# Expert products of a decoder trunk: column groups of 64 and 32 slots with plain fp32 weights in place of a three-product split

## The reference, cut to what matters

```
gu = xb @ w_gu[e] + b_gu[e]                  # 1024 -> 1024 (512 gate, 512 up)
gt = minimum(gu[:, :512], 7.0)
up = clip(gu[:, 512:], -7.0, 7.0)
act = gt * sigmoid(1.702 * gt) * (up + 1.0)
y = act @ w_down[e] + b_down[e]              # 512 -> 1024
```

## Time and profile before

| | |
|---|---|
| median of 3 runs | 1056.94 us (1056.68 to 1283.42) |
| the profiled execution | 1057.93 us |
| its span | 1056.1 us |
| TensorE busy | 996.8 us, 94% |
| VectorE busy | 778.8 us, 74% |
| ScalarE busy | 559.8 us, 53% |
| granted TensorE clock over the span | 0.98 |
| bytes moved by DMA | 283.35 MB |

### The profile page before, as it was taken

One profiled execution on the slowest core, in us unless ns is written; L12 is line 12 of the kernel. 1 busy time (PEld: TensorE's weight loads), 2 busy tenths in 40 slices (PEclk: granted clock), 3 DMA queues, 4 the chain that ended last, 5 costly groups with the idle time before them and its releaser, 6 DMA issues.

```text
span 1056.1 us, 13850 instructions
## 1 busy us (share of the span) xinstructions
PE 996.8 (94%) x4523; PEld 671.3 (64%) x4523; DVE 778.8 (74%) x1121; ACT 559.8 (53%) x840; POOL 215.2 (20%) x237
## 2 busy tenths in 40 slices
PE   3889999999999987899999999999999999999995
PEld 2566666667787557666666666666666666666652
DVE  0374967535534555898898898889989889898885
ACT  6334454452223233755575666756666665766742
POOL 1223931105100012212211212121122221212110
PEclk9899999999999998999999999999999999999998
DMA  9826624512316456889899999999999999999745
GB/s 343 297 81 239 239 81 168 188 43 70 118 69 239 159 206 235 307 310 316 307 332 370 360 370 366 351 373 359 369 357 354 377 354 363 368 365 363 245 126 195
DMA packets 63213, 283.35 MB, mean 268 GB/s; under 512 B 7489, under 2 KB 8797, under 8 KB 38601
## 3 DMA queue, kind: packets, MB, share of 16 engines
q1 hardware_dynamic: 53528, 257.93, 65.4%
q0 software_dynamic: 9648, 24.94, 8.9%
HBM read 272.62 MB, written 18.56 MB: 276 GB/s over the span
## 4 chain that ended last, share of the span: by engine, by line
PE 90%; DVE 5%; ACT 2%; issue 1%; DMA 1%; POOL 0%; ACTq 0%; SPq 0%; DVEq 0%
PE ps L1843 33%; PE ps L1578 19%; PE ps L1903 10%; PE ps L1897 9%; PE ps L1777 2%; PE ps L1607 2%; PE ps L1788 2%; PE ps L1626 2%; PE ps L1814 2%; PE ps L1692 2%; PE ps L1821 1%; PE ps L1864 1%; PE ps L1877 1%; DVE attn L1425 1%; DMA X<-in_x_dram 1%
## 5 line engine op out<-in xcount | busy, mean ns | idle before, releaser
L1843 PE MATMUL ps<-whl,xhl 128*96 128x512 f32 x1536 | 369.0, 399 | 0.0
L1307 DVE TENSOR_TENSOR whl<-ring,whl 128x1024 fp32r<-128x1024 f32 x256 | 304.4, 1221 | 52.5 <-ACT whl L965 51.8
L1843 PEld LDWEIGHTS ps<-whl,xhl 128*96 128x96 f32 x1536 | 249.8, 163 | 108.3 <-issue 0.2
L965 ACT ACTIVATE whl<-ring 128x1024 fp32r<-128x1024 f32 x256 | 268.2, 1061 | 63.7 <-PE ps L1843 43.9
L1578 PE MATMUL ps<-h_hi,wb_hl 128*128 128x512 f32 x384 | 127.1, 404 | 1.2 <-POOL wb_hl L652 1.2
L1903 PE MATMUL ps<-X,attn 128*96 128x512 f32 x256 | 115.4, 593 | 0.0
L733 POOL DMA_INDIRECT moe_rows<-mix,ius x31 | 46.3, 1493 | 304.8 <-ACT WC L1034 153.1
L1897 PE MATMUL ps<-whl,ahl 128*96 128x512 f32 x384 | 98.8, 407 | 2.9 <-DVE whl L1307 2.9
L1578 PEld LDWEIGHTS ps<-h_hi,wb_hl 128*128 128x128 f32 x384 | 72.9, 190 | 22.4 <-issue 5.2
L1307 DVE TENSOR_TENSOR whl<-X,whl 128x1024 fp32r<-128x1024 f32 x64 | 78.3, 1225 | 8.9 <-ACT whl L965 8.1
L965 ACT ACTIVATE whl<-X 128x1024 fp32r<-128x1024 f32 x64 | 67.8, 1062 | 20.0 <-PE ps L1843 20.0
(11 more groups left out here) (251 smaller groups left out, 1178.5 us busy)
## 6 DMA issues: line engine op xcount, KB each, us to landing
ring<-in_w_gu_dram SPq DMA_DIRECT2D x128, 1024.0 KB, 10.5
X<-in_w_down_dram SPq DMA_DIRECT2D x64, 1024.0 KB, 10.4
ring<-in_w_ada_dram SPq DMA_DIRECT2D x12, 2048.0 KB, 11.9
ring<-in_w_in_dram SPq DMA_DIRECT2D x6, 2048.0 KB, 7.8
ring<-in_w_out_dram SPq DMA_DIRECT2D x2, 2048.0 KB, 7.9
X<-in_x_dram SPq DMA_DIRECT2D x1, 2048.0 KB, 8.1
ring<-in_w_b_up_dram SPq DMA_DIRECT2D x1, 2048.0 KB, 14.8
ring<-in_w_a_up_dram SPq DMA_DIRECT2D x1, 2048.0 KB, 8.0
```

Source lines behind the costliest of these rows:

```text
L965: nc.scalar.activation(whl[:, buf, 0, :], part, ACT.Copy).then_inc(hi_ok, 1)
L1307: v.tensor_tensor(whl[:, buf, 1, :], part, whl[:, buf, 0, :], ALU.subtract).then_inc(lo_ok, 1)
L1843: last = mm(ps[0:slots, half, :], xhl[:, a, k, :], whl[:, at, b, half * CH:(half + 1) * CH], start=False, stop=(k == KD - 1 and a == 1))
```

## The change

An expert's products are all plain fp32, and nothing is split: `hi_part`, `lo_part`, `rows_low`, `act_low` and the ring `whl` are gone. The 96 slots are cut into 64 and 32. The first 64 are multiplied in two column groups of TensorE side by side (slots in output partitions 0 to 63 for one half of the columns, 64 to 127 for the other, 512 columns each), the last 32 in four groups (256 columns each). Each waits for a 1 MB half, does both of its blocks for the 64 slots, then both for the 32:

```diff
+            def up_pair(q, w):
+                w = w.rearrange("p (k u g c q) -> p k g c u q", k=2, u=2, g=2, c=2)
+                for i in range(2):
+                    k = 2 * q + i
+                    for g in range(2):
+                        mm(ps[SA * g:SA * (g + 1), 0, :], xgT[:, k, 0:SA], w[:, i, g, :, :, :], start=False,
+                           stop=(k == KD - 1), tile_position=(0, SA * g))
+                for i in range(2):
+                    k = 2 * q + i
+                    for j in range(4):
+                        last = mm(ps[SB * j:SB * (j + 1), 1, 0:2 * P], xgT[:, k, SA:slots], w[:, i, j // 2, j % 2, :, :],
+                                  start=False, stop=(k == KD - 1), tile_position=(0, SB * j))
+                return last
...
-                    for a, b in ((0, 0), (0, 1), (1, 0)):
-                        for half in range(2):
-                            last = mm(ps[0:slots, half, :], xhl[:, a, k, :], whl[:, at, b, half * CH:(half + 1) * CH],
-                                      start=False, stop=(k == KD - 1 and a == 1))
-                    last.then_inc(granule_used, 1)
```

`down_pair` does the same for the down weights, `biases` adds the bias once per group (2 matmuls of 512 columns, 4 of 256). Gate and up values now lie on 128 partitions x 384 columns instead of 96 x 512, so the three VectorE steps and the sigmoid run over 384 columns, and `turn_act` turns three 128 x 128 pieces. The result is weighed in six pieces:

```diff
-                for half in range(2):
-                    sl = slice(half * CH, (half + 1) * CH)
-                    last = v.scalar_tensor_tensor(out=Y[0:slots, b, sl], in0=ps[0:slots, 2 + half, :],
...
+                for g in range(2):
+                    sl = slice(g * CH, (g + 1) * CH)
+                    v.scalar_tensor_tensor(out=Y[0:SA, b, sl], in0=ps[SA * g:SA * (g + 1), 2, :], scalar=WC[0:SA, b:b + 1],
...
+                for j in range(4):
+                    sl = slice(j * 2 * P, (j + 1) * 2 * P)
+                    last = v.scalar_tensor_tensor(out=Y[SA:slots, b, sl], in0=ps[SB * j:SB * (j + 1), 3, 0:2 * P],
```

The weights have sixteen 1 MB places (`half_home`) in one ring, gate-up and down alike, and a place is free when its products are done (`half_used`). The rows of a down half are taken so that each partition gets two pieces of 4 KB instead of one of 8 KB:

```diff
-            dn = w_down[0, bass.ds(e, 1), :, :].rearrange("a (p k) n -> p (a k n)", k=KF)
-            return dn[:, q * PAIR:(q + 1) * PAIR]
+            dn = w_down[0, bass.ds(e, 1), :, :].rearrange("a (k p) n -> p (a k) n", k=KF)
+            return dn[:, 2 * q:2 * q + 2, :]
```

More of the change, by code:

```diff
@@ L553, in _, with refill @@
[L553 to L564 removed]
+            def refill(e, r):
+                for q in range(4):
+                    sp.wait_ge(half_used, up_no(e, q) - NH + 1)
+                    load_up(e, q, r * PER - 2 + q)
+                for q in range(2):
+                    sp.wait_ge(half_used, down_no(e - 1, q) - NH + 1)
+                    load_down(e - 1, q, r * PER + 2 + q)
@@ L1816, in turn_rows, with biases @@
                 last.then_inc(done, 1)
-            def biases(e, half):
+            def biases(b):
                 pe.wait_ge(b3_ok, 1)
-                mm(ps[0:slots, half, :], sel3[:, bass.ds(e, 1)].broadcast_to([3 * NE, slots]), b3[:, half * CH:(half + 1) * CH],
-                   start=True, stop=False)
-            def up_whole(e, done):
-                for half in range(2):
-                    biases(e, half)
-                    for k in range(KD):
-                        last = mm(ps[0:slots, half, :], xgT[:, k, :], gu_part(0, k)[:, half * CH:(half + 1) * CH], start=False,
-                                  stop=(k == KD - 1))
-                    last.then_inc(done, 1)
@@ new lines, in came, with up, down @@
+            def came(n, rounds):
+                pe.wait_ge(half_in[n % NH], rounds * 48 + n // NH * 16 + 16)
+            def up(e, r, rounds=0):
+                biases(r % 2)
+                for q in range(4):
+                    n = q if isinstance(e, int) and e == 0 else r * PER - 2 + q
+                    came(n, rounds)
+                    up_pair(q, half_home(n)).then_inc(half_used, 1)
+            def down(e, r, rounds=0):
+                for q in range(2):
+                    n = down_no(e, q) if isinstance(e, int) else r * PER + 8 + q
+                    came(n, rounds)
+                    down_pair(q, half_home(n)).then_inc(half_used, 1)
@@ L1953, in _ @@
                         pe.wait_ge(ov_w, n * 96 + 96)
-                        up_whole(e, ov_gu)
+                        biases(0)
+                        for q in range(4):
+                            last = up_pair(q, half_home(q))
+                        last.then_inc(ov_gu, 1)
                         pe.wait_ge(ov_av, n + 1)
@@ L1957, in _ @@
                         pe.wait_ge(ov_at, n + 1)
-                        down(ov_dn)
+                        for q in range(2):
+                            last = down_pair(q, half_home(4 + q))
+                        last.then_inc(ov_dn, 1)
                 pe.wait_ge(ov_y, OVER * NE)
```

367 lines of the change are left out of this document (139 added, 228 removed).

## The result

The changed kernel takes 1064.16 us (median of 6 runs, 1062.65 to 1069.28), the kernel before in the same comparison 1057.34 us (median of 6). One run of the kernel before took 1283.42 us and is left out of the ratio, which compares the means of the others: 1.0074, with a 95% interval of 1.0044 to 1.0103, within 2%, though not nothing. The profiled execution of the changed kernel is its slowest, 1069.28 us with a span of 1067.5; against the span of 1056.1 before there are 11.4 us to find.

A forecast was written before the change was run, and what follows sets the result against it. TensorE was taken to set the pace, with DMA also full. Period +10.3, places waits -2.6 and tail -3.0 gave +4.7 us: 1062.6 on the profiled execution, forecast 1062 us, range 1012 to 1095 us.

The forecast's parts named there:

- The period: TensorE's time per expert in the loop: 19.05 us against 18.72, +10.3 us over 31 periods and the last gate-up.
- rival D: Column groups in TensorE's products don't run fully side by side: 320 us more, or 1187 us in a milder form; chance 0.04.
- B (cheap changes): The 12 changes between 64 and 32 per expert don't drain TensorE: 17.85 us per expert, 1024 us; chance 0.28.
- C: At each of 16 changes TensorE's next group waits for the last record's whole tail, 0.16 us: 1092 us; chance 0.20.
- The sum without changes: TensorE's products, biases and transposes per expert, before any cost for changing group size: 16.74 us.
- The places products wait 0.65 us for VectorE in experts 1 to 4: At the loop's start, these TensorE waits were taken as gone with the splits: -2.6 us.
- The tail: From the last gate-up's end to the last weighing: products and turning -4.9 us, weighing +1.9, net -3.0 us.
- The weighing grows from two pieces to six, but nobody waits for it until the tail: Weighing of each expert's result: hidden in the loop, 3.2 us against 1.41 in the tail, +1.9 us.
- The bound on the 4 KB pieces: Down-half loads in 4 KB instead of 8 KB pieces: between no loss and 0.3 us per expert.
- DMA could follow no faster for long: In the kernel before, DMA was held to be full too, at share 1.00 and 363 GB/s, while TensorE set the pace.
- The floor of 17.5 us: DMA's least time per expert, with loads running ahead: remaining 203 MB take 559 us at 363 GB/s.
- What stays hidden: Activation steps, 3.8 us, stay covered by TensorE's transposes and 5.7 us of down products; losing that costs some 2 us per expert.

The follow-up runs named there:

- the direct pair: Changed kernel without the 32 slots' products, down halves in 4 KB pieces against 8 KB pieces: 1019.15 and 1001.42 us.
- the three together: Changed kernel with pairs in turned order (11 changes), TensorE's loop written out and the last expert's result in its own banks: 1031.93 us, ratio 0.9763.
- the other two edits: Against the changed kernel, tried singly: TensorE's expert loop written out, 1059.73 us; last expert's down products in PSUM banks of their own, 1063.96 us.
- the one with the other tail: Changed kernel with the last expert's down products in PSUM banks 4 and 5, without the wait for weighing expert 30: 1063.96 us, ratio 1.0043.
- the three with other orders: Changed kernel with group sizes taking turns at every block, every four blocks, or pairs in turned order: 1121.88, 1035.53 and 1040.42 us.

## Why the prediction was right, point by point

The time, 1062 us for 1064.16, is closer than its parts, and that is luck.

**The period** held: 19.05 forecast, 19.06 measured. (Its terms, 16.74 and 7 x 0.15, 7 x 0.12 and 2 x 0.20, add to 19.03.) Two groups of 64 run fully side by side, which no row had shown: rival D is out. The change between 64 and 32, which also no row had shown, costs 0.15 and 0.14 us, where I took 0.15 and 0.12 from the changes to and from other widths. The runs with 28, 11, 10 and 8 changes show the price as one per change. Every change is paid, so B (cheap changes) is out, and the 0.177 us from which C decides is not reached. These runs agree with the Trainium skill's rule in "TensorEngine Tiling (Array Packing)", section Tiling Modes, that a change of mode drains the engine: each one costs 0.144 us here. The sum without changes, 16.74 us, stands against 16.76 by the line.

**The start of the loop** failed in size. I counted 6 x 0.33 of period and took the places waits at -2.6 us, so about -0.6; measured -7.2. The step that failed is "The places products wait 0.65 us for VectorE in experts 1 to 4": it took one wait per expert from one row, where the waits view has six of them, 4.2 us, and behind expert 0's biases two more for a split and an activation, 2.4 us. Of these 6.6 us none remained but 1.0 for an activation, and 0.6 for a load of rows came in. That is 2.4 us of the miss of 6.6. Half clock behind the waits is 3.3 more: before, 13.01, 12.99 and 4.54 us for 11.43, 11.43 and 2.99, 4.7 us in all, after it 1.4. The last 0.9 us are not split up.

**The turn of the loop** was not in the sum at all: +6.6 us in the profiled execution, 4.4 by the medians without it. I read TensorE's program as a list. That its code has to be loaded when it jumps, and that the changed kernel's body is eight experts where the one before had two, was a step the prediction missed. In the trace before no such gap stands between 556 and 990 us. The mechanism (the code is fetched again at the jump) rests on the written-out loop, on "issue", and on the instruction packets: none in 560 to 980 us with the body of two experts, 29 with eight. The kernels without the 32 slots' products settle it, since they keep the loop of eight experts with 65 matmul records to an expert instead of 161. In 650 to 820 us, which holds their jump back, their instruction queue moves nothing, and no wait with "issue" stands in 500 to 960 us. So the stall comes with the length of the body in instructions; where the limit lies, between 520 and 1288 records, no run shows.

**The tail** failed in sign: -3.0 forecast, +3.4 measured. The failed step is "The weighing grows from two pieces to six, but nobody waits for it until the tail", which then went on to count only the last weighing there. The last down product waits for the weighing before it, because both use the same banks. Before, a split was later than that and hid it. The sum: 2.6 us of wait, 1.6 us of half clock behind it, 1.6 us of half clock in the last product behind the 3.7 us of weighing, and 0.3 us of weighing over the 3.2 counted: 6.1 of the 6.4 between forecast and measurement. (3.2 less 1.41 is 1.8, where the prediction has 1.9.) Weighing itself was well taken (748 and 481 ns for 710 and 450).

**DMA**: that it follows and does not bound was right, and so was the sign of the landing times. The bound on the 4 KB pieces, "no loss, and some 5% on a third of the bytes, 0.3 us per expert", is open: the direct pair gave 0.63, the 366 and 368 GB/s of other kernels with the same pieces far less. The step "DMA could follow no faster for long" took a share of 1.00 and 363 GB/s, at which TensorE set the pace, for what DMA can do; the three together ran 25 experts at 18.34 us without a wait for a load. The floor of 17.5 us by the lead was about right: with the 358 to 368 GB/s measured, 203 MB take 552 to 567 us, 17.2 to 17.7 per expert, and 17.91 still ran without a wait.

**What stays hidden** in the loop stayed hidden: no wait for ScalarE or VectorE from expert 6 to the last, with VectorE busy 38% of the span and ScalarE 22%.

So the total came out by cancelling. Measured less forecast, the first six experts are -6.6 us, experts 6 to 30 +5.9 (14.2 against 25 x 0.33), the tail +6.4 and the front +1.1: together the 6.7 us between 1062.6, the forecast for a profiled execution, and 1069.28. Between the medians, 1064.16 and the forecast 1062, 2.2 are left.

## What to carry to other kernels

Count the changes of column-group size on TensorE, not only the slots: here each cost 0.144 us, so the order of the same products alone decided between 6% slower (28 changes) and 2.1% faster (10), and with the other two edits 3.7% faster (8). When a limiting step is removed at the end of a program, ask what else its consumer waits for, reused banks above all, and what clock it then restarts with. And a total that agrees says nothing of its parts: split the span at the same markers before and after, and check each term.

## What was unexpected of the hardware

- A loop body of eight experts on TensorE stalls where it jumps back, 4.95 us in this kernel, 4.81 in the one with the other tail, 4.49, 4.48 and 3.23 in the three with other orders, and the clock behind it is at half. A body of two experts (164 matmul records) and one of eight shorter experts (520) did not stall, and their instruction queues moved nothing around the jump; the body of eight here has 1288. The Trainium skill has this, in "Runtime: NRT & Kernel Launch", section Instruction fetch mechanics: a taken branch out of what is held costs a fetch. The run with the loop written out agrees.
- A DMA share of 1.00 does not say that the engines are at their limit: 358 GB/s showed 1.00, and 368 GB/s of the same traffic 1.01.
- Half clock did not come from every gap: in the tail, behind 0.58 us of idle time the next part took 1.94 us, behind 3.18 us 3.04.
